# Sparse attention block: one panel's three steps moved between the stretches of a hand-written order

## The chip, the cores and the metric

The kernel runs on one core of one Trainium2 chip. The metric is the device time of one execution in microseconds (us). TensorE (PE) does the matrix products and the transposes, VectorE (DVE) and ScalarE (ACT) the elementwise work, GpSimd (POOL) a part of it, and SyncE (SP) issues most transfers. Each engine works through its own queue in the order in which the program was written; semaphores make an instruction wait for another engine.

## What is computed

The reference is a stack of two blocks with two layers each, all for 512 tokens of width 1024. The change lies in the second block, whose layer (it is run twice) is this, cut to what matters here:

```python
proj = h @ w_in
(q, k, v, g_att, qi, ki, wi, z, xbc, dt_raw, gl_att, gl_ssd) = _split_cols(proj, IN_SIZES)
...
# one_block of _dsa_attention, 128 queries at a time
dots = jnp.einsum('bqhd,bsd->bqhs', qib, ki32) * IDX_DIM ** -0.5          # 4 index heads
score = jnp.einsum('bqhs,bqh->bqs', jax.nn.relu(dots), wb)
score = jnp.where(admissible[None], score, NEG)
_, sel = lax.top_k(score, topk)                                           # topk = 128
logits = ...(q, k[sel]) ; p = softmax(logits) ; o = p @ v[sel]            # 8 heads
y_att = (o_att * jax.nn.silu(g_att)) @ w_branch_a
...
xbc = jax.nn.silu(_causal_dwconv(xbc, conv_w, conv_b))                    # 12 chunks of 128 columns
y = _ssd_chunked(...)
```

## The kernel before

All arrays are kept transposed, 128 columns of a projection on the partitions and the 512 tokens along the free axis. Weights stream through a ring in **panels**: a panel is the 128 output columns of one projection chunk, 8 tiles of 128x128. Each panel is split into a high part (L566, always on ACT) and a low part (L570, on DVE or on POOL), and multiplied in three products per tile, so one panel is 24 matmuls `bank<-hT,wparts 128x512` (L458) into one PSUM bank. `pe_linear_steps` cuts these into three **steps** of 9, 9 and 6 matmuls.

Each layer of the second block (`block2`) has one long stretch in which three **strands** are interleaved. Every strand gives each engine a sequence of steps.

- Strand 0, the projections: four query panels (13 steps), one step for the time constants, five convolution panels (15 steps), then the seven late convolution panels woven with six small steps of `before` (27 steps: the transposes `nat`, the product `last` that reads `rstd`, and for each of two groups the products `cb`, four 128x128 blocks, and the transposes `bn`), then four gate panels (12 steps), and last one step `late_silu`, on ACT alone. A convolution panel costs ACT its start (L1136) and DVE three taps (L1145, together one tap set), a gate panel costs ACT one copy (L2378). `late_silu` is a table load, seven activations (L2140) and four (L2143).
- Strand 1, the selection: for query tiles 1 to 3 the index scores (L2201 on ACT, L2216 and L2219 on DVE) and the search for the 128 largest, which is 16 **rounds** of MAX8 and MATCH_REPLACE8 (L2232, L2234) on DVE for each tile and a mask (L2238) at its end. The width of a round is 256, 384 and 512 for tiles 1, 2 and 3.
- Strand 2, the attention (`softmax_maps`): 32 **maps**, eight heads for each of four query tiles, 128, 256, 384 and 512 keys wide, in 35 steps. PE computes the scores of two maps at once (`bank<-arena 64x..`, then the mask products with `cb_sb`), DVE takes the maximum (L831), ACT the exponential (L819), PE transposes (L468), ACT copies the transposed map out of PSUM (L811; for every fourth map DVE does it, L843), PE multiplies by the values (`last_bank<-arena`), and DVE scales the result out of its single bank (L857). Scores and transposes share four banks, so the scores of a pair wait until both exponentials of the pair before are done. The masks of tile 1 are needed from map 8 on, those of tile 2 from map 16, those of tile 3 from map 24.

The order of the strands is written out by hand as a list of strand numbers. `alternate` walks through it and takes the next step of that strand on all four engines at once; `spread(a, b, c)` deals out a, b and c steps of strands 0, 1 and 2 evenly over a stretch. All the engines' queues follow from this list. The stretches are: four pairs of steps, then the index scores with the search for tile 1 and four rounds of that for tile 2 (strands 0 and 1 only), then the rest of the search for tile 2 beside the maps 0 to 7 (**stage A**), then the search for tile 3 beside the maps 8 to 15 (**stage B**), then the last nineteen map steps (**stage C**).

After the stretch `pe_ot` (L468) transposes the attention output and waits for the last map's result (`"out", 31`); DVE multiplies it with the gates (L2447), then comes `pe_ssd`, which transposes `xbc` into banks that DVE drains (L2561).

Of the kernel before, what the change touches and what calls it, by code (L numbers as in the profile page):

```python
# [253 lines left out]
def spread(*counts):  # L254

    return [i for _, i in sorted(((step + 0.5) / n, i) for i, n in enumerate(counts) for step in range(n))]


def alternate(order, *parts):

    def program(functions):
        def run(eng):
            steps = [f(eng) if f else (i for i in ()) for f in functions]
            for i in order:
                next(steps[i], None)
            for rest in steps:
                finish(rest)
        return run
    return [program([p[i] if i < len(p) else None for p in parts]) for i in range(4)]
# [84 lines left out]
def build(nc, ins, out, known=None, final=False):  # L354
# [9 lines left out]
    with ExitStack() as ctx:  # L364
# [809 lines left out]
        def then(parts=None, **kw):  # L1174
            if parts is not None:
                for e, f in zip(("act", "pe", "dve", "pool"), parts):
                    prog[e].append(f)
            for e, f in kw.items():
                prog[e].append(f)
# [499 lines left out]
        order = [PROJECT, PROJECT, PROJECT, COMPRESS, COMPRESS] * 4  # L1679
# [288 lines left out]
        order = [0, 0, 0] + spread(6, 8) + spread(9, 8) * (KD - 2) + [0] + [1] * (len(maps) + 3)  # L1968
# [55 lines left out]
        def block2(l, nxt, hfree, arena_free):  # L2024
# [404 lines left out]
            rounds, ahead = TOPK // 8, 4  # L2429
            first = 3 * len(later) + 2 + 3 * EARLY - 4  # L2430
            order = [1, 0] * 4 + spread(first, 8 + rounds + ahead)
            order += spread(3 * 5 + 4, rounds - ahead, 8) + spread(3 * 4 + 2, rounds, 8) + spread(3 * 2 + 1, 0, 19)
            then(alternate(order, *strands))

            def pe_ot(pe):
# [355 lines left out]
            return mg  # L2791

        block2(0, Norm("L1h", 0), filled[("f1", "b"), FC - 1], filled[("f1", "y"), KD - 1])
        mg1 = block2(1, None, filled["L0gls", KD - 1], filled["L0out", KD - 1])

        A = Area()
# [209 lines left out]
```

## Time and profile before

| | us |
|---|---|
| median of 3 runs | 2464.34 (2463.07 to 2464.41) |
| profiled execution, its own time | 2462.13 |
| its span on the core | 2460.3 |
| PE busy | 2391.7 (97% of the span) |
| DVE busy | 1423.8 (58%) |
| ACT busy | 1019.4 (41%) |
| POOL busy | 273.9 (11%) |

The median lies 4.0 us above the span and 2.2 us above the profiled execution. The interleaved stretch of the first of the two layers is at 1480 to 1646 us, that of the second about 510 us later. PE is busy nearly all the time, so what can be won or lost is the time in which it waits, plus the time in which its clock is granted at half.

### The profile page before, as it was taken

The numbers are of one execution on the slowest core, as the hardware profiler recorded it, in microseconds if no ns is written. First come the engines' busy times: TensorE is split into PE (matmuls) and PEld (weight loads), VectorE is DVE, ScalarE is ACT, GpSimd is POOL, SyncE is SP. The second block draws the span as 40 slices with busy tenths as digits, with TensorE's granted clock in tenths as the row PEclk, the third lists the DMA queues.
The fourth block names the chain that finished last, engine by engine and source line by source line (L and its number), as shares of the span: only waits on it lengthen the run. The fifth ranks groups of instructions, "written<-read, shape, count | busy, mean of one in ns | idle before, by whom it ended". The sixth has DMA issues, their size and how long they took to land.

```text
span 2460.3 us, 32007 instructions
## 1 busy us (share of the span) xinstructions
PE 2391.7 (97%) x12074; PEld 1925.8 (78%) x12086; DVE 1423.8 (58%) x2366; ACT 1019.4 (41%) x1732; POOL 273.9 (11%) x260
## 2 busy tenths in 40 slices
PE   8999999999999999999999999989999999999998
PEld 7877788888887888788888866777888777678886
DVE  3545655655655666566456469947533578566333
ACT  3656654322334444443233334444422354445223
POOL 0000111000000000100000236302100233011001
PEclk9999999999999999999999999999999999999999
DMA  5211002433432111134334312201232221102321
GB/s 205 87 51 44 1 27 97 152 141 115 147 124 91 60 57 56 61 111 146 145 112 150 107 60 69 69 27 39 92 97 92 79 74 61 43 27 78 103 95 52
DMA packets 58039, 211.77 MB, mean 86 GB/s; under 512 B 6432, under 2 KB 6560, under 8 KB 57888
## 3 DMA queue, kind: packets, MB, share of 16 engines
q1 hardware_dynamic: 57456, 208.86, 24.7%
q8 instruction: 99, 1.62, 0.3%
q10 hardware_dynamic: 432, 0.85, 0.1%
q14 instruction: 52, 0.43, 0.1%
HBM read 207.60 MB, written 2.10 MB: 85 GB/s over the span
## 4 chain that ended last, share of the span: by engine, by line
PE 84%; DVE 6%; issue 4%; ACT 4%; POOL 1%; DMA 0%; SPq 0%; ACTq 0%; DVEq 0%; POOLq 0%
PE bank L458 77%; PE last_bank L458 5%; PE bank L468 3%; DVE arena L1145 1%; DVE arena L2232 1%; ACT wparts L566 1%; DVE arena L2234 1%; DVE small L831 1%; ACT arena L819 1%; POOL rstd L625 0%; DVE wparts L570 0%; DMA ring<-weights_dram 0%; ACT arena L2140 0%; DVE arena_r L584 0%; DVE arena L1006 0%
## 5 line engine op out<-in xcount | busy, mean ns | idle before, releaser
L458 PE MATMUL bank<-hT,wparts 128*128 128x512 f32 x5568 | 1341.3, 397 | 6.9 <-ACT hT L693 4.5
L458 PEld LDWEIGHTS bank<-hT,wparts 128*128 128x128 f32 x5568 | 1038.2, 189 | 239.8 <-issue 24.9
L570 DVE TENSOR_TENSOR wparts<-ring,wparts 128x1024 fp32r<-128x1024 f32 x290 | 366.7, 1265 | 427.0 <-ACT wparts L566 426.8
L458 PE MATMUL bank<-arena_r,wparts 128*128 128x512 f32 x2400 | 566.1, 396 | 0.0
L458 PEld LDWEIGHTS bank<-arena_r,wparts 128*128 128x128 f32 x2400 | 450.1, 188 | 108.4 <-DVE arena_r L600 0.3
L566 ACT ACTIVATE wparts<-ring 128x1024 fp32r<-128x1024 f32 x332 | 348.2, 1049 | 162.1 <-PE bank L458 130.9
L819 ACT ACTIVATE arena<-bank,small 128x128 f32<-128x128 f32 (+3 forms) x192 | 100.9, 526 | 143.0 <-DVE small L831 141.8
L468 PE MATMUL bank<-cf_sb,arena 128*128 128x128 f32 (+1 forms) x816 | 132.8, 281 | 16.7 <-DMA cf_sb<-cf_dram 4.9
L458 PE MATMUL last_bank<-arena 128*128 128x64 f32 x972 | 133.0, 273 | 7.3 <-DVE arena L854 3.1
L458 PEld LDWEIGHTS last_bank<-arena 128*128 128x128 f32 x972 | 124.2, 195 | 16.1 <-issue 9.8
L831 DVE TENSOR_REDUCE small<-bank 128x1 f32<-128x128 f32 (+3 forms) x192 | 93.3, 486 | 57.8 <-PE bank L458 46.2
L570 POOL TENSOR_TENSOR wparts<-ring,wparts 128x1024 fp32r<-128x1024 f32 x42 | 101.1, 2409 | 213.1 <-ACT wparts L566 213.1
L468 PEld LDWEIGHTS bank<-cf_sb,arena 128*128 128x128 f32 (+1 forms) x816 | 96.9, 148 | 32.4 <-DVE arena L1006 5.1
L596 ACT ACTIVATE arena_r<-arena 128x512 fp32r<-128x512 f32 x68 | 42.9, 631 | 179.9 <-POOL arena L2785 93.7
L625 POOL TENSOR_TENSOR rstd<-hv 128x512 f32<-128x512 f32 x6 | 7.8, 1294 | 939.8 <-ACT hv L615 939.8
L458 PE MATMUL bank<-arena 128*64 128x128 f32 (+6 forms) x708 | 91.4, 329 | 14.0 <-ACT arena L819 13.6
L811 ACT ACTIVATE arena<-bank 128x384 f32<-128x384 f32 (+3 forms) x136 | 58.0, 426 | 112.4 <-PE bank L468 111.6
L1136 ACT ACTIVATE arena<-arena,vecs 128x512 f32<-128x512 f32 x44 | 36.0, 817 | 147.3 <-DVE arena L1821 147.3
L458 PEld LDWEIGHTS bank<-arena 128*128 128x128 f32 (+2 forms) x708 | 63.5, 170 | 29.6 <-ACT arena L819 16.2
L1145 DVE SCALAR_TENSOR_TENSOR arena<-arena,vecs 128x511 f32<-128x511 f32 x88 | 66.0, 751 | 16.6 <-ACT arena L1136 15.1
L458 PE MATMUL bank<-cb_sb 128*128 128x128 bf16 (+2 forms) x372 | 74.5, 256 | 0.2
L1821 DVE TENSOR_TENSOR arena<-bank,rstd 128x512 f32<-128x512 f32 x44 | 30.4, 691 | 66.6 <-PE bank L458 62.2
(274 smaller groups left out, 2103.4 us busy)
## 6 DMA issues: line engine op xcount, KB each, us to landing
ring<-weights_dram SPq DMA_DIRECT2D x388, 512.0 KB, 3.4
arena<-x_dram SPq DMA_DIRECT2D x4, 512.0 KB, 5.8
out_dram<-arena SPq DMA_DIRECT2D x4, 512.0 KB, 4.0
rot<-rot_dram SPq DMA_DIRECT2D x1, 512.0 KB, 10.4
rot<-rot_dram ACTq DMA_DIRECT2D x1, 512.0 KB, 3.2
cf_sb<-cf_dram SPq DMA_DIRECT2D x1, 416.0 KB, 8.8
cb_sb<-cb_dram SPq DMA_DIRECT2D x1, 264.0 KB, 9.6
vecs<-vec_dram ACTq DMA_DIRECT2D x1, 258.5 KB, 6.1
```

Source lines behind the costliest of these rows:

```text
L458: i = pe.matmul(*args, **kw)
L468: i = pe.transpose(*args)
L566: eng.activation(wparts[:, slot, 0, :, :], ring[:, p % RAW, :, :], ACT.Copy)\
L570: eng.tensor_tensor(wparts[:, slot, 1, :, :], ring[:, p % RAW, :, :], wparts[:, slot, 0, :, :].bitcast(F32), ALU.subtract)\
L596: act.activation(dst, src, ACT.Copy).then_inc(*act_made.mark((key, "hi")))
L811: act.activation(PT[:, j % 3, 0:W], banks[key, "t", j][:, 0:W], ACT.Copy)\
L819: act.activation(Pb[:, i % 3, 0:W], banks[key, "s", i][:, 0:W], ACT.Exp, bias=mx(i), accum_out=sm(i)).then_inc(*act_made.mark((key, "p", i)))
L831: dve.tensor_reduce(mx(i), banks[key, "s", i][:, 0:W], AX.X, ALU.max, negate=True)\
L1136: act.activation(cv, src, ACT.Identity, bias=b, scale=w).then_inc(*act_made.mark((key, "tap", n)))
L1145: dve.scalar_tensor_tensor(out=cv[:, s:SEQ], in0=src[:, 0:SEQ - s], scalar=w, in1=cv[:, s:SEQ], op0=ALU.mult, op1=ALU.add)\
L1821: dve.tensor_tensor(an[:, n % 3, :], banks[(key, "a"), n][:, :], scale, ALU.mult)\
L2232: dve.max(tops[:, r, :], sc).then_inc(*dve_made.mark((K + "top", qt, r)))
```

## The change

One line of the order list. The four counts of strand 0 over the stretches were 25, 19, 14 and 7; they are now 25, 22, 14 and 4. Three steps, which is one panel, leave stage C and enter stage A. Since strand 0 is a sequence, everything behind its 48th step shifts: stage A takes three more steps of the woven part, stage B begins three steps later in that sequence and takes nine gate steps in place of six, and stage C has three gate steps and `late_silu` in place of six and `late_silu`.

```diff
-            order += spread(3 * 5 + 4, rounds - ahead, 8) + spread(3 * 4 + 2, rounds, 8) + spread(3 * 2 + 1, 0, 19)
+            order += spread(3 * 6 + 4, rounds - ahead, 8) + spread(3 * 4 + 2, rounds, 8) + spread(3 * 1 + 1, 0, 19)
```

In PE matmuls of width 512 the stages held 120, 87 and 48; now they hold 135, 96 and 24. No instruction is added or removed.

**PE, the start of stage A.** Before, the second score pair (`bank<-arena 128x128 x2`) and a transpose stand ahead of the product `last` (`bank<-rstd,cf_sb`):

```order
L458 MATMUL bank<-hT,wparts 128x512 x24
L458 MATMUL bank<-arena 128x128 x2
L458 MATMUL bank<-cb_sb 128x128 x2
L468 MATMUL bank<-cf_sb,arena 128x128
L458 MATMUL bank<-rstd,cf_sb 128x64
L458 MATMUL bank<-hT,wparts 128x512 x6
L468 MATMUL bank<-cf_sb,arena 128x128
L458 MATMUL last_bank<-arena 128x64
```

Now:

```order
L458 MATMUL bank<-hT,wparts 128x512 x24
L458 MATMUL bank<-rstd,cf_sb 128x64
L458 MATMUL bank<-arena 128x128 x2
L458 MATMUL bank<-cb_sb 128x128 x2
L468 MATMUL bank<-cf_sb,arena 128x128
L458 MATMUL bank<-hT,wparts 128x512 x24
L468 MATMUL bank<-cf_sb,arena 128x128
L458 MATMUL last_bank<-arena 128x64
```

The score pair now stands behind `last`, and 24 matmuls of projection stand between two map steps where 6 stood.

**DVE, the end of stage A.** Before, the fifth tap set of the late panels comes behind the mask of tile 2 (L2238):

```order
L831 TENSOR_REDUCE small<-bank 128x1
L836 RECIPROCAL small<-small 128x1
L843 COPY arena<-bank 128x128
L857 TENSOR_SCALAR arena<-last_bank,small 128x64
L2232 MAX arena<-arena 128x8
L2234 MATCH_REPLACE arena<-arena 128x384
L2238 TENSOR_SCALAR arena<-arena 128x384
L1145 SCALAR_TENSOR_TENSOR arena<-bank,vecs,arena 128x511
L1145 SCALAR_TENSOR_TENSOR arena<-bank,vecs,arena 128x510
L1145 SCALAR_TENSOR_TENSOR arena<-bank,vecs,arena 128x509
```

Now:

```order
L1145 SCALAR_TENSOR_TENSOR arena<-bank,vecs,arena 128x511
L1145 SCALAR_TENSOR_TENSOR arena<-bank,vecs,arena 128x510
L1145 SCALAR_TENSOR_TENSOR arena<-bank,vecs,arena 128x509
L2232 MAX arena<-arena 128x8
L2234 MATCH_REPLACE arena<-arena 128x384
L831 TENSOR_REDUCE small<-bank 128x1
L836 RECIPROCAL small<-small 128x1
L843 COPY arena<-bank 128x128
L857 TENSOR_SCALAR arena<-last_bank,small 128x64
L2232 MAX arena<-arena 128x8
L2234 MATCH_REPLACE arena<-arena 128x384
L2238 TENSOR_SCALAR arena<-arena 128x384
```

A tap set has moved ahead of the mask, and behind the mask comes a round of the next search.

**ACT, the end of stage C.** Before, both last copies of transposed maps (maps 30 and 31, `x2`) stand ahead of `late_silu`:

```order
L819 ACTIVATE arena,small<-bank,small 128x512
L2378 ACTIVATE arena<-bank 128x512
L819 ACTIVATE arena,small<-bank,small 128x512
L811 ACTIVATE arena<-bank 128x512 x2
L2140 ACT_TABLE_LOAD
L2140 ACTIVATE arena<-arena 128x512 x7
L2143 ACTIVATE arena<-arena 128x512 x4
L566 ACTIVATE wparts<-ring 128x1024
```

Now:

```order
L819 ACTIVATE arena,small<-bank,small 128x512 x2
L811 ACTIVATE arena<-bank 128x512
L2140 ACT_TABLE_LOAD
L2140 ACTIVATE arena<-arena 128x512 x7
L2143 ACTIVATE arena<-arena 128x512 x4
L811 ACTIVATE arena<-bank 128x512
L566 ACTIVATE wparts<-ring 128x1024
```

The copy of map 31 now stands behind the whole of `late_silu`. Both layers are ordered alike.

## Rows read from the trace of the kernel before

**Rows 1.** The page, part 1: busy time, share of the span, instructions

```profile
PE 2391.7 (97%) x12074; PEld 1925.8 (78%) x12086; DVE 1423.8 (58%) x2366; ACT 1019.4 (41%) x1732; POOL 273.9 (11%) x260
```

**Rows 2.** PE's waits, total, times, longest: 1520 to 1660, then 2032 to 2172

```profile
PE bank L458 <- ACT arena L819: 6.8, 7, 2.0
...
PE bank L458 <- ACT arena L819: 6.7, 7, 2.0
```

**Rows 3.** Windows: busy PE, PEld, DVE, ACT, POOL; clock; DMA; stages A, B, C

```profile
1522.08:1562.79 40.71, 36.93 (x188) 28.75 (x187) 34.50 (x89) 20.55 (x42) 14.82 (x9) 0.96 0.16 54
1562.79:1597.33 34.54, 31.41 (x165) 24.56 (x164) 33.57 (x83) 12.14 (x30) 9.41 (x4) 0.95 0.19 62
1597.33:1646.66 49.33, 44.12 (x279) 33.23 (x280) 21.24 (x60) 23.58 (x55) 0.00 (x0) 1.00 0.10 33
```

**Rows 4.** Timeline of PE in stage A: start, us, instruction, idle before

```profile
1536.25 0.40 PE L458 MATMUL bank<-rstd,cf_sb 16*128 16x64 f32 x2 [3.20 <-DVE arena L1145]
...
1554.72 4.36 PE L458 MATMUL bank<-hT,wparts 128*128 128x512 f32 x18
```

**Rows 5.** Timeline of DVE: tap set, mask, round, ninth maximum, low part

```profile
1554.44 2.32 DVE L1145 SCALAR_TENSOR_TENSOR arena<-bank,vecs,arena 128x511 f32<-128x511 f32 x3 [2.19 <-ACT arena L1136]
...
1561.27 1.45 DVE L2238 TENSOR_SCALAR arena<-arena 128x384 bf16<-128x384 f32 x1
...
1566.83 0.68 DVE L2232 MAX8 arena<-arena 128x8 f32<-128x512 f32 x1
...
1569.74 0.42 DVE L831 TENSOR_REDUCE small<-bank 128x1 f32<-128x256 f32 x1
...
1622.03 1.23 DVE L570 TENSOR_TENSOR wparts<-ring,wparts 128x1024 fp32r<-128x1024 f32 x1 [1.24 <-ACT wparts L566]
```

**Rows 6.** Timeline of PE: score pairs of maps 8, 10, 12, 14 and 18

```profile
1562.79 0.70 PE L458 MATMUL bank<-arena 64*128 64x256 f32 x4
...
1570.90 0.77 PE L458 MATMUL bank<-arena 64*128 64x256 f32 x4 [1.99 <-ACT arena L819]
...
1580.49 0.70 PE L458 MATMUL bank<-arena 64*128 64x256 f32 x4
...
1589.52 0.70 PE L458 MATMUL bank<-arena 64*128 64x256 f32 x4 [1.14 <-ACT arena L819]
...
1603.39 0.92 PE L458 MATMUL bank<-arena 64*128 64x384 f32 x4 [1.35 <-ACT arena L819]
```

**Rows 7.** Timeline of PE: score pairs of maps 22, 26, 28 and 30

```profile
1612.78 0.92 PE L458 MATMUL bank<-arena 64*128 64x384 f32 x4 [0.31 <-ACT arena L819]
...
1624.81 1.13 PE L458 MATMUL bank<-arena 64*128 64x512 f32 x4 [1.27 <-ACT arena L819]
...
1631.15 1.13 PE L458 MATMUL bank<-arena 64*128 64x512 f32 x4
...
1635.98 1.13 PE L458 MATMUL bank<-arena 64*128 64x512 f32 x4 [0.35 <-ACT arena L819]
```

**Rows 8.** Timeline of ACT: copy of map 31, then the step `late_silu`

```profile
1643.67 0.60 ACT L811 ACTIVATE arena<-bank 128x512 f32<-128x512 f32 x1 [0.95 <-PE bank L468]
1644.29 1.28 ACT L2140 ACT_TABLE_LOAD   x1
1645.58 3.75 ACT L2140 ACTIVATE arena<-arena 128x512 f32<-128x512 f32 x7
1649.24 2.17 ACT L2143 ACTIVATE arena<-arena 128x512 f32<-128x512 f32 x4
```

**Rows 9.** Timeline of PE: values of map 31, transposes behind the maps

```profile
1645.21 1.08 PE L458 MATMUL last_bank<-arena 128*128 128x64 f32 x8 [0.47 <-DVE arena L857]
1646.66 6.59 PE L468 MATMUL bank<-cf_sb,arena 128*128 128x128 f32 x44 [0.38 <-DVE arena L857]
1654.28 0.66 PE L468 MATMUL bank<-cf_sb,arena 128*128 128x128 f32 x4 [1.02 <-DVE arena L2561]
```

**Rows 10.** Windows of PE alone: busy, granted clock, after the wait of rows 6

```profile
1572.00:1574.00 2.00, 2.00 (x8) 0.50 0.00 0
```

## Prediction

> **What bounds the kernel now.** The page's busy shares come first: PE is busy 97% of the span, the others far less [rows 1]. The amount of work doesn't change, so the time can change only by PE's waits and by stretches in which its clock is granted at half. Next I looked for PE's waits in the interleaved stretch; the list of waits names the exponentials of ACT as the largest, 6.8 us in seven waits in one layer and 6.7 us in the other [rows 2], so the two layers may be treated alike. Then the windows by stage. In A, PE is busy 36.93 of 40.71 us and DVE 34.50; in B, PE 31.41 of 34.54 and DVE 33.57, 97%; in C, PE 44.12 of 49.33 and DVE only 21.24 [rows 3]. So DVE ends the waits in B, in A both are close, and C is a chain of short dependences between PE, DVE and ACT in which projection matmuls fill holes. The change takes 24 matmuls out of C, puts 15 into A and 9 into B.
>
> **The unit.** 18 projection matmuls last from 1554.72 to 1558.92, where the next instruction starts, 4.2 us [rows 4], so 0.233 us each and 5.6 us for a panel.
>
> **Stage A: 4.9 us longer on PE, mask 5.5 us later.** PE waits 3.20 us for a bank that a tap set must drain, until 1536.25 [rows 4]. That tap set hangs on earlier work of ACT and POOL that keeps its order, so I leave 1536.25 where it is; the score pair that now comes behind the wait (0.55 us, from 1532.23 to 1532.78 by the same timeline) is work moved behind it. From there to the scores of map 8 PE now has 102 matmuls of width 512, 23.8 us; 1.7 us lost to the half clock that follows this wait as it does now; and small pieces of 6.0 us: `last`, three score pairs at about 0.6, two `cb` products at 0.86, `bn` at 0.4, five transposes with values at 0.25. That ends at 1567.7, where it ended at 1562.79 [rows 6]: 4.9 later, made of 3.5 for 15 matmuls, 0.86 for a `cb` that comes forward, 0.55 for the score pair. DVE gets a fifth tap set in this stage, 2.2 us, and idles more, since each tap set waits for ACT's convolution start and that for the end of PE's panel: already now one such wait is 2.19 us [rows 5]. The panels end on PE at 1553.6 and 1560.7; the fifth tap set starts 0.8 us behind the latter, at 1561.5. Behind it come a round (1.2), the small operations of a map (0.65), a round (1.24) and the mask (1.45), all with the durations of now. The mask ends at 1568.25, where it ended at 1562.7 [rows 5].
>
> **Stage B and the first pair of C: 0.8 us shorter (bounds 1.3 and 0.3).** DVE leads here. Behind the mask stand a round of width 512 (1.5), a tap set (2.2), a map's maximum and small operations (0.6), two rounds (2.9, from 1566.83 to 1569.74 [rows 5]). The ninth maximum so starts at 1575.45. Now the scores of map 10 start 1.16 us behind it (1569.74 to 1570.90 [rows 5, 6]); then they start at 1576.6. PE alone could start them at 1574.05 (8.11 us less the wait of 1.99, three more matmuls, `bn` in place of `cb`). So the wait grows from 1.99 to about 2.55. The next tap set needs a panel that PE ends at 1579.5 to 1580.5 and starts at 1580.3 to 1581.3; with two rounds and 1.16 behind it the scores of map 12 start at 1586.6 to 1587.6. To those of map 14 it is 9.03 us now with 1.14 of wait [rows 6]; DVE has one tap set less between them, so I take 7.9. Then 7.8 as now, and to the scores of map 18 6.06 less the wait of 1.35, since the low part that stood between the two maxima (1.23 us on DVE [rows 5]) has moved ahead of them: 4.7. They start at 1607.0 to 1608.0, for 1603.39: **+3.6 to +4.6**, I take +4.1.
>
> **Stage C from map 18 on: -6.0 us.** The 24 matmuls leave, -5.6. What a pair costs bare is shown by two cycles that have no filler: the pair of map 22 waits 0.31 us, that of map 30 0.35 us and comes 4.83 us behind that of map 28 [rows 7]. Four cycles will be bare where two are, so about 0.7 us of new wait. In return the wait of 1.27 us before map 26 goes [rows 7]: it came from a panel's high part on ACT and low part on DVE in that cycle, which now stand elsewhere; and one of 0.40 us before map 24, where ACT's gate copy stood ahead of the exponential. Sum -5.6 + 0.7 - 1.67, which is -6.6; by walking the pairs one by one I get -6.0 and take that. Bounds -5.0 (a bare cycle costs twice as much) and -6.6.
>
> **The end of C: +3.2 us.** `late_silu` lasts from 1644.29 to 1651.41, 7.1 us, and the copy of map 31 stood ahead of it [rows 8]; now it stands behind. Count from the scores of map 30. Now, with six matmuls between (1.4 us, which are gone), the copy of map 30 ends at 6.7, so 5.35 without them. `late_silu` then ends at 12.5, the copy at 13.0, PE takes the values of map 31 at 13.15, having stood from 7.35 on: **a new wait of 5.8 us**. The transposes of `pe_ot` start 1.45 us behind the values (1645.21 to 1646.66 [rows 9]), at 14.6. Of 44 transposes each takes 0.11 us unless it waits, 4.9, so the next four come at 19.5; before they came at 18.3 (1654.28 less 1635.98 [rows 7, 9]), less 1.4. That is +2.6. Why so little: those transposes already ran behind `late_silu`, since the gate products, the low part and the drains of DVE come behind it, and PE waits 1.02 us for that at 1654.28 [rows 9]. The other bound is the half clock. A wait of 1.99 us is enough today for 0.50 in the window behind it, in which eight matmuls take two microseconds [rows 6, 10]; a wait of 5.8 us should do so too, and half-rate transposes add up to 1.1: +3.7. I take +3.2.
>
> **Sum.** Per layer 4.1 - 6.0 + 3.2 = +1.3, for two layers +2.6. The span goes from 2460.3 to 2462.9, the median, 4.0 above it, from 2464.3 to **2466.9**.
>
> **A rule of the Trainium skill that speaks for more.** The trace shows 1.28 us for the table load in `late_silu`, and the first activation starts 0.01 us behind it [rows 8]; nothing stands between the copy's end and the load either. The Trainium skill, "ScalarE: Activation LUTs", section What ACT_TABLE_LOAD costs, adds a drain of about 1.38 us to a load of 1.28 for each switch. By that rule, an estimate, the copy of map 31 would come 1.4 us later per layer and the sum would be +5.4 in place of +2.6. The trace contradicts it for this load.
>
> **Rivals.**
>
> *The holes of A and B take the panel (faster).* If DVE idles less in A than I count, the three waits of 1.99, 1.14 and 1.35 [rows 6] vanish, together with the half clock behind the first (1.7 us). A and B then cost 5.6 - 4.5 - 1.7 = -0.6, the layer -0.6 - 6.0 + 3.2 = -3.4, the kernel 2457.5. For it: PE's share of work grows between the maps, so DVE has more time for each maximum. Against: the fifth tap set stands ahead of the mask, and DVE is busy 97% of B [rows 3].
>
> *DVE carries its whole delay through B (slower).* The mask is 5.5 us late. If B costs DVE all of its 35.5 us again (the tap set that left, 2.2, is made up by the low part, 1.2, and by the wait for the panel, 1.0 or more) the scores of map 18 start 6 us late in place of 4.1; with -5.0 in C and +3.7 at its end the layer is +4.7, the kernel 2473.7. It decides once DVE waits more than about 2 us for the tap set at 1580. For it: every stage has its own slowest engine now, PE in A and DVE in B, and what one gives up the other doesn't take. Against: B needs 34.4 us of DVE where it needed 35.5.
>
> *The change doesn't hurt the tail.* If the copy of map 31 isn't waited for, because the transposes behind it are held by something else anyway, the layer is 4.1 - 6.0 = -1.9 and the kernel 2460.5. Against it stands the order alone: `pe_ot` waits for the output of map 31, and PE can't go around it.
>
> **How the numbers follow.** The forecast as summed, within the bounds of its terms (3.6 - 6.6 + 2.6 = -0.4 to 4.6 - 5.0 + 3.7 = +3.3 a layer, 2463.5 to 2471), has 0.6. The slower rival has 0.22, the faster one 0.1, the harmless tail 0.08. The table rule lies within the forecast's range and has 0.05 of those 0.6. About 0.2%, 4.9 us, is what a measurement of this kernel can tell from no change: 2459.4 and 2469.3 are the borders. Of the forecast a sixth lies above 2469.3, with the slower rival 0.3; the faster rival lies almost wholly below 2459.4, and so does a sliver of the harmless tail, 0.1; 0.6 remains for no difference. The range goes from 2461.5, which leaves out the faster rival and some of the harmless tail, to 2472.5, which takes in half of the slower one.
>
> **What would show it.** In the changed profile: the scores of map 8 about 5 us later and the mask of tile 2 5 to 6 us later; a wait of 2 to 3 us before the scores of map 10; no wait over 0.5 us before those of maps 24 and 26; the scores of map 18 3.6 to 4.6 us later; and a wait of 5 to 6 us on PE for ACT's L811 once per layer, with a window at 0.50 near it. The prediction is wrong in its first part if the wait before map 10 is gone, in its last if the wait behind map 30 is short. The three terms have opposite signs and each is larger than their sum, so the sign of the whole is its weakest part.

## The result

The changed kernel takes 2471.94 us (median of 8 runs, 2467.45 to 2476.75), the kernel before 2464.38 us (8 runs, 2463.07 to 2465.94) in the same comparison. The ratio is 1.003 with a 95% interval from 1.0021 to 1.0039: slower by 7.6 us. The forecast was 2466.9, with a range from 2461.5 to 2472.5; it called a difference under 0.2% the likeliest, and that is not what came. The measured time lies inside the range, 0.6 us below its upper end.

The profiled execution of the changed kernel took 2467.45 us, which is its fastest run. Its span is 2465.6 us. The page, part 1, for [rows 1]:

```profile
PE 2388.7 (97%) x12086; PEld 1922.9 (78%) x12086; DVE 1424.6 (58%) x2366; ACT 1019.6 (41%) x1732; POOL 273.9 (11%) x260
```

As before, PE is busy 97% of the span, and these shares don't show the change. The list of PE's waits of the interleaved stretch, first layer, does (engine, line waited for: total, times, longest; for [rows 2]):

```profile
PE last_bank L458 <- ACT arena L811: 5.7, 1, 5.7
PE bank L458 <- ACT arena L819: 5.3, 7, 1.3
PE bank L458 <- DVE arena L1145: 4.5, 2, 4.0
```

The waits for exponentials fell from 6.8 to 5.3 us, and a single wait of 5.7 us for a copy (L811) is new. Windows of the changed kernel (columns as in [rows 3]): from the first score pair to that of map 8, from there to map 18, to map 30, and to the first matmul of the next panel behind the maps:

```profile
1519.27:1564.60 45.33, 40.80 (x211) 32.55 (x210) 36.99 (x92) 21.30 (x43) 17.05 (x9) 0.96 0.21 71
1564.60:1604.97 40.37, 36.23 (x192) 27.47 (x191) 35.66 (x89) 16.63 (x39) 7.18 (x3) 1.00 0.16 54
1604.97:1632.87 27.90, 25.91 (x168) 18.64 (x168) 13.50 (x40) 13.01 (x34) 0.00 (x0) 1.00 0.06 21
1632.87:1656.19 23.32, 17.21 (x111) 15.31 (x111) 9.53 (x20) 11.17 (x20) 1.03 (x1) 0.78 0.05 15
```

The last three of these stretches of the kernel before (the first is the first of [rows 3], 40.71 us):

```profile
1562.79:1603.39 40.60, 36.12 (x191) 28.08 (x191) 37.25 (x91) 15.68 (x38) 9.41 (x4) 0.96 0.21 67
1603.39:1635.98 32.59, 29.63 (x183) 21.85 (x186) 13.95 (x40) 13.95 (x35) 0.00 (x0) 1.00 0.09 31
1635.98:1655.07 19.09, 17.02 (x116) 14.66 (x117) 8.77 (x19) 11.79 (x21) 1.03 (x1) 0.91 0.03 6
```

I call these four stretches A, B', C' and the end in what follows; B' reaches one pair further than B, to map 18. The differences are +4.62, -0.23, -4.69 and +4.23 us: +3.9 for the layer, and by the same marks +4.1 in the second layer, 8.0 together. The two spans differ by only 5.3, since the execution of before that was profiled came 2.8 us later to the start of the stretch (1522.08 against 1519.27), where both kernels are alike. A second profile of the changed kernel has the stretch start at 1525.15, takes 137.05 us for the layer in place of 136.92, and has a span of 2471.6. So the sum over the layers, not the difference of two spans, is what answers to the medians. The same marks in all thirteen profiles bear this out: what comes behind the second of these stretches takes 293.9 us in each (293.85 to 293.99), while the first stretch, which the same program precedes in all, starts anywhere from 1519.27 to 1525.29.

### The profile page after: what moved, and what is told of

It is laid out like the page before. It is cut to its first block, busy times and chain, and to the rows that moved or that the text cites. A ratio compares the mean times of both kernels' runs of the same rounds, so it can differ in the third digit from the quotient of the medians.

```text
span 2465.6 us, 32019 instructions
## 1 busy us (share of the span) xinstructions
PE 2388.7 (97%) x12086; PEld 1922.9 (78%) x12086; DVE 1424.6 (58%) x2366; ACT 1019.6 (41%) x1732; POOL 273.9 (11%) x260
## 4 chain that ended last, share of the span: by engine, by line
PE 84%; DVE 6%; issue 4%; ACT 4%; POOL 1%; DMA 0%; SPq 0%; ACTq 0%; DVEq 0%; POOLq 0%
PE bank L458 76%; PE last_bank L458 4%; PE bank L468 3%; DVE arena L1145 1%; DVE arena L2232 1%; DVE arena L2234 1%; DVE small L831 1%; ACT arena L819 1%; ACT wparts L566 0%; POOL rstd L625 0%; DMA ring<-weights_dram 0%; DVE wparts L570 0%; ACT arena L2140 0%; DVE arena_r L584 0%; ACT arena L1136 0%
## 5 line engine op out<-in xcount | busy, mean ns | idle before, releaser
L570 DVE TENSOR_TENSOR wparts<-ring,wparts 128x1024 fp32r<-128x1024 f32 x290 | 366.7, 1265 | 427.3 <-ACT wparts L566 427.1
L570 POOL TENSOR_TENSOR wparts<-ring,wparts 128x1024 fp32r<-128x1024 f32 x42 | 101.2, 2412 | 206.0 <-ACT wparts L566 205.9
L811 ACT ACTIVATE arena<-bank 128x384 f32<-128x384 f32 (+3 forms) x136 | 57.9, 426 | 102.5 <-PE bank L468 101.7
L1145 DVE SCALAR_TENSOR_TENSOR arena<-arena,vecs 128x511 f32<-128x511 f32 x88 | 66.0, 750 | 16.6 <-ACT arena L1136 15.1
```

The lines of the kernel that those rows point to most:

```text
L570: eng.tensor_tensor(wparts[:, slot, 1, :, :], ring[:, p % RAW, :, :], wparts[:, slot, 0, :, :].bitcast(F32), ALU.subtract)\
L811: act.activation(PT[:, j % 3, 0:W], banks[key, "t", j][:, 0:W], ACT.Copy)\
L1145: dve.scalar_tensor_tensor(out=cv[:, s:SEQ], in0=src[:, 0:SEQ - s], scalar=w, in1=cv[:, s:SEQ], op0=ALU.mult, op1=ALU.add)\
```

## The end of C in the changed kernel

Timeline of PE, from the scores of map 30 on (start, us, instruction, idle before; for [rows 9]):

```profile
1632.87 1.13 PE L458 MATMUL bank<-arena 64*128 64x512 f32 x4 [0.35 <-ACT arena L819]
...
1639.37 1.08 PE L458 MATMUL last_bank<-arena 128*128 128x64 f32 x8
1646.10 1.97 PE L458 MATMUL last_bank<-arena 128*128 128x64 f32 x8 [5.65 <-ACT arena L811]
1648.44 7.99 PE L468 MATMUL bank<-cf_sb,arena 128*128 128x128 f32 x48 [0.38 <-DVE arena L857]
1656.19 4.14 PE L458 MATMUL bank<-hT,wparts 128*128 128x512 f32 x17
```

And ACT beside it, for [rows 8]:

```profile
1637.84 0.60 ACT L811 ACTIVATE arena<-bank 128x512 f32<-128x512 f32 x1 [0.29 <-PE bank L468]
1638.45 1.28 ACT L2140 ACT_TABLE_LOAD   x1
1639.75 3.74 ACT L2140 ACTIVATE arena<-arena 128x512 f32<-128x512 f32 x7
1643.40 2.17 ACT L2143 ACTIVATE arena<-arena 128x512 f32<-128x512 f32 x4
1645.47 0.57 ACT L811 ACTIVATE arena<-bank 128x512 f32<-128x512 f32 x1
```

PE stands from the values of map 30 until the copy of map 31, which is queued behind all of `late_silu`. The eight matmuls of map 31 then take 1.97 us where those of map 30 took 1.08, and the 48 transposes take 7.99. The windows of PE alone, for [rows 10], inside the wait, behind it in three places, and in the next panel (length, busy, granted clock, DMA share, GB/s):

```profile
1644.00:1646.00 2.00, 0.00 (x0) 0.50 0.00 0
1646.40:1648.40 2.00, 1.67 (x8) 0.50 0.03 8
1648.40:1651.40 3.00, 2.96 (x14) 0.50 0.00 0
1651.40:1654.40 3.00, 3.00 (x19) 0.62 0.00 0
1654.60:1657.60 3.00, 3.00 (x23) 1.00 0.52 175
```

The clock is at its lower level, 1.2 GHz (0.50; the upper one is 2.4 GHz, 1.00), already within the wait and stays there through most of the transposes: 14 of them in three microseconds. So the order of ACT's queue costs twice: the wait, and the work behind it at half rate.

## Experiments

Ahead of each result stands what was written before that run. The runs came in three groups, each with its own runs of the kernel before; their medians are 2463.9 (the changed kernel once more, both moves of `late_silu`, the filled wait), 2464.2 (the panel from C into B, both moves of rounds, 16, 14, 10) and 2464.8 (the last three). Differences are taken within a group.

### The changed kernel once more

> The changed kernel once more, as the partner of the three runs beside it. In its profile the layer is 3.9 us longer than before: +4.4 up to the scores of map 18, -5.9 from there to the end of map 30's values, +5.4 from there to the first z panel. My theory (the copy of map 31 behind late_silu, and the half clock that the 5.65 us wait brings) expects about +8 us on the median, that is 2472, and each layer's stretch with the clock at 0.50 near the end of the maps. The rival theory (what costs is the delay of DVE in the stages A and B) expects the same time but for another reason.

2472.59 us (5 runs), ratio 1.0035 [1.0022, 1.0048], 8.7 above before. The result repeats. The profiled run of these is the one of 2471.6 us of span named above.

### The same order with late_silu behind the last map step

```diff
             order += spread(3 * 6 + 4, rounds - ahead, 8) + spread(3 * 4 + 2, rounds, 8) + spread(3 * 1 + 1, 0, 19)
+            order += [order.pop(len(order) - 1 - order[::-1].index(0))]
```

> The changed order with its last projection step (late_silu) put back behind the last map step; only ACT's order differs from the changed kernel. My theory: the wait of 5.65 us before the values of map 31 is gone, from the end of map 30's values to the first z panel it takes 10.3 us again instead of 15.7, a layer is 4.4 - 5.9 = -1.5 against before, the kernel 2461.4 us (2460 to 2463), 3 us faster than before. The rival (A and B carry the loss): 2468 to 2472, since nothing in A and B differs from the changed kernel.

2463.47 us (11 runs), ratio 0.9996 [0.9988, 1.0005]: 9.1 us below the changed kernel, though the panel is still in A. That is 0.5 above its range, of which the ledger below tells, and far from the rival's 2468. The end of this kernel on PE, whose scores of map 30 start at 1637.25:

```profile
1646.76 1.97 PE L468 MATMUL bank<-cf_sb,arena 128*128 128x128 f32 x16 [0.38 <-DVE arena L857]
1649.68 3.50 PE L468 MATMUL bank<-cf_sb,arena 128*128 128x128 f32 x28 [0.96 <-ACT arena L2140]
1654.38 0.66 PE L468 MATMUL bank<-cf_sb,arena 128*128 128x128 f32 x4 [1.20 <-DVE arena L2562]
1655.18 5.72 PE L458 MATMUL bank<-hT,wparts 128*128 128x512 f32 x24
```

The transposes still wait for `late_silu` (0.96 and 1.20 us), but sixteen of them run before that wait, at full rate, and the end takes 17.93 us in place of 23.32. A and B' are as long as in the changed kernel. The whole slowdown hangs on which of two ACT steps comes first.

### The kernel before with late_silu ahead of the copy of map 31

```diff
             order += spread(3 * 5 + 4, rounds - ahead, 8) + spread(3 * 4 + 2, rounds, 8) + spread(3 * 2 + 1, 0, 19)
+            order.insert(len(order) - 3, order.pop(len(order) - 2))
```

> The order of before with late_silu put one map step earlier, so that the copy of map 31 stands behind it; nothing is moved between the stages. My theory: PE waits 5 to 6 us before the values of map 31 in each layer, and with the half clock a layer is 5.4 us longer: 2464.4 + 10.8 = 2475 us (2470 to 2477). The rival: the transposes behind the maps wait for late_silu anyway, so at most +1 a layer, 2464 to 2466.

2472.84 us (5 runs), ratio 1.0039 [1.0026, 1.0051]. This is the end of the change alone, with every panel where it was:

```profile
1652.65 1.97 PE L458 MATMUL last_bank<-arena 128*128 128x64 f32 x8 [5.65 <-ACT arena L811]
1655.00 7.39 PE L468 MATMUL bank<-cf_sb,arena 128*128 128x128 f32 x48 [0.38 <-DVE arena L857]
```

The same wait of 5.65 us and the same 1.97. Against the same kernel with `late_silu` last this order alone costs 9 us, within the theory's range and far from the rival's 1 us a layer. By the layer it costs 4.8 us here (23.91 for 19.09) and 5.4 in the changed kernel (23.32 for 17.93): the values come as late in both, but here the clock is back earlier, and from the transposes to the next panel it is 7.15 us in place of 7.75.

### The wait filled with matmuls

For map 31 (`fill_at=31` in the call for these 32 maps) PE takes the bank of its values first, then runs 26 matmuls into it whose results nobody reads (they are overwritten), then waits for the copy. The order of the other engines is that of the changed kernel.

```diff
-        def softmax_maps(..., together=False, busy=0):
+        def softmax_maps(..., together=False, busy=0, fill_at=None):
...
+                        if j and j == fill_at:
+                            bank = banks.take(pe, (key, "o", j), out)
+                            pe_busy(pe, bank, 26)
...
-                        if j:
+                        if j and j != fill_at:
```

> The changed kernel with 26 matmuls of width 512 (bf16, result overwritten) put on PE into the wait before the values of map 31, so that PE has work in it; they add no time unless they last longer than the wait of 5.65 us. Theory of the clock (half of the loss at the end of the maps is the half clock that the wait brings): no window at 0.50 behind the maps, the end of stage C costs 2.6 to 3 us instead of 5.4, the kernel 2466.5 us (2465 to 2468). The rival, that the order alone costs the 5.4: the kernel stays at 2472.

2466.02 us (11 runs), ratio 1.0014 [1.0005, 1.0023], 6.6 us below the changed kernel, with work added. Its end on PE, and the window over its transposes:

```profile
1644.37 5.56 PE L458 MATMUL last_bank<-cb_sb 128*128 128x512 bf16 x25 [0.61 <-DVE arena L860]
1649.76 1.00 PE L458 MATMUL last_bank<-arena 128*128 128x64 f32 x8
1651.14 5.69 PE L468 MATMUL bank<-cf_sb,arena 128*128 128x128 f32 x48 [0.38 <-DVE arena L860]
1656.98 1.40 PE L458 MATMUL bank<-hT,wparts 128*128 128x512 f32 x5
```

```profile
1651.20:1656.20 5.00, 4.99 (x45) 1.00 0.00 0
```

(The trace has 25 of the 26; a few matmul records can be missing from a trace.) ACT's copy comes as late as before, and the values of map 31 start even later, 13.58 us behind the scores of map 30 for 13.23, since the last of the filler is still running. But from there to the transposes it is 1.38 us in place of 2.34, and from the transposes to the next panel 5.84 in place of 7.75. The instructions and their number are the same and the clock is 1.00 in place of 0.50, so the half clock costs 1.0 and 1.9, together 2.9 us a layer. The end takes 20.80 us (1636.18 to 1656.98) in place of 23.32. The rest of the end's cost is the order itself: 23.32 less 2.9 and less the 17.93 with `late_silu` last, 2.5 us a layer.

### The panel from C into B

```diff
-            order += spread(3 * 5 + 4, rounds - ahead, 8) + spread(3 * 4 + 2, rounds, 8) + spread(3 * 2 + 1, 0, 19)
+            order += spread(3 * 5 + 4, rounds - ahead, 8) + spread(3 * 5 + 2, rounds, 8) + spread(3 * 1 + 1, 0, 19)
+            order += [order.pop(len(order) - 1 - order[::-1].index(0))]
```

> The panel leaves stage C as in the change, but goes wholly into stage B (19, 17 and 4 steps of strand 0), and late_silu stands behind the last map step. Stage A is that of the kernel before. Theory (the cost of the change ahead of the scores of map 18 comes from putting the panel into A, in front of the mask): A stays at 40.7 us, B takes the panel partly into its three waits of 1.99, 1.14 and 1.35 us, so from the scores of map 8 to those of map 18 it is 42 to 43.5 us where it is 40.6 before; C loses 5.9, its end nothing. The layer is 2 to 4 us shorter than before, the kernel 2456 to 2460. Rival (a panel costs its full 5.6 us wherever it stands, since maximum, exponential and search form one chain whose waits come back): B is 46 us, the kernel 2463 to 2465, like the change with late_silu last.

2457.03 us (6 runs), ratio 0.9971 [0.9959, 0.9982]: faster than before by 7.1 us and than the changed kernel by 15, as its theory says; the rival's 2463 to 2465 didn't come. The windows of B' and the end (A and C' are in the ledger):

```profile
1560.22:1603.07 42.85, 40.46 (x216) 31.21 (x215) 38.20 (x92) 16.85 (x40) 9.35 (x4) 1.00 0.22 74
1630.96:1648.88 17.92, 14.70 (x111) 11.93 (x111) 8.67 (x19) 11.30 (x20) 1.03 (x1) 1.00 0.03 5
```

B' had 4.48 us of idle PE (40.60 less 36.12) and a mean clock of 0.96; now it has 2.39 idle and the full clock. Of the panel's 5.6 us only 2.25 show: 2.1 went into idle time, and the rest, 1.3, is what the full clock gives back. A keeps its length, and C' saves the same 4.7 as in the change.

### Two rounds of the third search from B into A

The changed kernel with `late_silu` last, and then the kernel before, each with `rounds - ahead + 2` and `rounds - 2` in the first two stretches. PE's order doesn't change by it.

> The changed kernel with late_silu behind the last map step, and two of the sixteen rounds of the search for tile 3 (1.45 us of DVE each) moved from stage B into stage A, whose PE order stays as it is. Theory (DVE leads in B, PE in A): in A DVE is busy 37.0 of 45.3 us and takes the 2.9 us into its idle time, so A grows by 0 to 1 us; in B the three waits of 1.3, 1.3 and 1.15 us shrink by 2 to 2.9 us together. The layer is 1 to 2.9 us shorter, the kernel 2458 to 2461.5 where it is 2463.5 without this edit. Rival (DVE's work from the start of A to the end of B is one chain with the panels, and a round costs the same wherever it stands): no change, 2462.5 to 2464.5; or the mask and the first maxima of B come 2.9 us later and the kernel is 2465 to 2469.

> The kernel before with the same edit as the run before this but one: two rounds of the search for tile 3 moved from stage B into stage A. Theory (DVE leads in B already before the change): in A DVE has 6.2 us of idle time and PE 3.8; A grows by 0.5 to 2 us, B loses 2 to 2.9 of its 4.5 us of waits, the layer is 0 to 2 us shorter, the kernel 2460 to 2464. If DVE's work in A and B is one chain, nothing changes, 2464. If this edit gains less here than on the changed kernel, the panel in A has indeed given DVE idle time there that it lacks before.

On the changed order 2463.47 us (11 runs), ratio 0.9993 [0.9984, 1.0002], where 2463.47 was measured without the edit; on the order of before 2462.46 (11 runs), ratio 0.9995 [0.9986, 1.0003]. The windows of B' in the changed order without the two rounds' move, and with it:

```profile
1568.95:1609.36 40.41, 36.24 (x192) 27.47 (x191) 35.69 (x89) 16.65 (x39) 7.19 (x3) 1.00 0.17 54
```

```profile
1569.46:1610.02 40.56, 36.18 (x192) 27.48 (x192) 34.07 (x84) 16.52 (x39) 7.18 (x3) 1.00 0.17 55
```

DVE is busy 1.6 us less, not the 2.9 of two rounds, and B' doesn't get shorter. Part of the difference is the mask of tile 2, which took 0.36 us in the changed order and takes 1.52 here (the last section comes back to it). The mask, and two waits in B', one of PE and one of DVE:

```profile
1562.85 1.52 DVE L2238 TENSOR_SCALAR arena<-arena 128x384 bf16<-128x384 f32 x1
...
1574.82 0.41 PE L458 MATMUL last_bank<-arena 128*128 128x64 f32 x2 [1.30 <-DVE arena L857]
...
1582.36 2.32 DVE L1145 SCALAR_TENSOR_TENSOR arena<-bank,vecs,arena 128x511 f32<-128x511 f32 x3 [1.97 <-ACT arena L1136]
```

The tap set at 1582.36 waits 1.97 us for its panel, where the same one waits 1.05 in the changed kernel: DVE had time to spare there. And PE waits 1.30 us for a small operation of DVE (L857) where it had no wait. On the order of before:

```profile
1564.20:1603.88 39.68, 34.76 (x191) 26.88 (x191) 34.25 (x85) 15.68 (x38) 9.41 (x4) 1.00 0.20 66
```

DVE is busy 3.0 us less than in B' of before and the stretch is 0.92 shorter, while the clock goes from 0.96 to 1.00 and PE's busy time falls by 1.36. A did not grow but fell by 0.23. The time lies in the range of its theory, but not for its reason: B' should have lost 2 to 2.9 us of waits. So the total of DVE's work doesn't set the length of B'. On the changed order the time is that of the rival, no change; its reason, one unbroken chain of DVE's work, doesn't fit the 1.97 us in which DVE stands idle. The mask blurs both tests by 1.1 us, since it got longer by that in the one and shorter in the other.

### More and other panels

Counts of strand 0 over A, B and C, `late_silu` last in all three: 16, 14, 10; then 19, 20, 1; then 16, 20, 4.

> The opposite move: one panel leaves stage A and enters C (16, 14 and 10 steps of strand 0 where before has 19, 14 and 7), late_silu behind the last map step. Theory (A has PE as its slowest engine, C is a chain with holes): C takes 5.6 us of matmuls, of which 0.7 to 1 fill bare pairs, so +4.5 to +5.5; in A and B the scores of map 18 come 3 to 4.4 us earlier, less than a panel, since DVE is busy 34.5 of 40.7 us in A and 97% of B. The layer is 0.5 to 2 us longer than before, the kernel 2465 to 2468. Rival (the exchange is even, as between before and the changed kernel with late_silu last): 2463 to 2465.

> One more panel leaves stage C for stage B (19, 20 and 1 steps of strand 0, late_silu last; the version with 19, 17 and 4 gave 2457.0). Theory (a panel is cheap only while the stage that takes it has idle time on PE, and worth removing only while its stage isn't bare): B has 2.4 us of idle PE left in 42.85, so the panel adds 4.5 to 6 us there; C loses only 2 to 3 us, since then all of its pairs are bare chains of 3.7 to 4.9 us. The layer is 1.5 to 4 us longer, the kernel 2460 to 2465. Rival (the gain of 7 us repeats, B still hides part of it): 2450 to 2456.

> One panel from C and one from A both into stage B (16, 20 and 4 steps of strand 0, late_silu last). Theory (idle PE time in B is used up by the first panel): A takes 37.3 us as in the run with 16 steps there, 3.4 less than with 19; B takes 47 to 48.5 where it is 42.85; the layer is 0.7 to 2.2 us longer than with 19, 17 and 4, the kernel 2458 to 2462. Rival (B is the stage with room, and a panel costs less there than anywhere else): 2453 to 2456.5.

They take 2467.36 us (11 runs), ratio 1.0013 [1.0004, 1.0021]; 2458.53 us (9 runs), 0.9979 [0.9970, 0.9989]; and 2458.04 us (11 runs), 0.9973 [0.9964, 0.9982]. None is below 2457.03, though the last two, measured in another group, can't be told from it. The first lies in its expectation as a whole, with both parts smaller: C' grew by 4.2 (4.5 to 5.5 expected), and the scores of map 18 came 2.7 earlier (3 to 4.4). The third has A and B' as its theory says (37.32 and 47.76). The second is better than its theory's 2460 to 2465 and short of its rival's 2450 to 2456. Its B':

```profile
1564.87:1610.90 46.03, 43.70 (x231) 34.16 (x230) 38.79 (x92) 17.69 (x41) 9.44 (x4) 1.00 0.24 81
```

C' fell by 2.41, to 25.48, as expected, and has no panel left. But B' grew by 3.2 and not by 4.5 to 6, because I had counted 24 matmuls where 15 enter it (231 instructions on PE for 216): the nine of the first step of C stand between the maps 16 and 18 already and so within B'. 15 matmuls of 0.233 are 3.5 us; B' hid next to nothing of them, and C' gave back 2.4 for them, 1.1 less than they take.

### The panel in B, late_silu in the changed kernel's place

> Steps 19, 17 and 4 of strand 0, but late_silu ahead of the last map step as in the changed kernel. Theory (the cost of the end of C is independent of where the panel went): the new wait of 5.7 us, half clock for 10 us behind it, 3.5 to 4.6 us a layer, so 7 to 9 us above the version with late_silu last: 2464 to 2466. Rival (late_silu costs little when ACT arrives early at the end of C): under 2461.

2465.75 us (11 runs), ratio 1.0004 [0.9995, 1.0013], 8.7 above the version with `late_silu` last, in the range of its theory. The wait of 5.65 us and the half clock come wherever the panel goes; the end costs 4.8 us here (22.70 for 17.92), as on the order of before, where it is 5.4 in the changed kernel.

### The ledger

All in us, first layer; the two columns on the right are both layers together and the measured medians, each less before.

| counts of A, B, C | `late_silu` | A | B' | C' | end | layer | two layers | measured |
|---|---|---|---|---|---|---|---|---|
| 19, 14, 7 (before) | last | 40.71 | 40.60 | 32.59 | 19.09 | 132.99 | 0 | 0 |
| 22, 14, 4 (the change) | early | 45.33 | 40.37 | 27.90 | 23.32 | 136.92 | +8.0 | +7.6 |
| 22, 14, 4 | last | 45.33 | 40.41 | 27.89 | 17.93 | 131.56 | -2.4 | -0.4 |
| 19, 14, 7 | early | 40.76 | 40.60 | 32.58 | 23.91 | 137.85 | +8.9 | +9.0 |
| 22, 14, 4, wait filled | early | 45.36 | 40.43 | 27.89 | 20.80 | 134.48 | +2.3 | +2.1 |
| 19, 17, 4 | last | 40.73 | 42.85 | 27.89 | 17.92 | 129.39 | -7.1 | -7.1 |
| 19, 17, 4 | early | 40.74 | 42.84 | 27.89 | 22.70 | 134.17 | +1.8 | +1.0 |
| 22, 14, 4, rounds moved | last | 45.69 | 40.56 | 27.89 | 17.93 | 132.07 | -1.7 | -0.7 |
| 19, 14, 7, rounds moved | last | 40.48 | 39.68 | 32.59 | 19.09 | 131.84 | -2.3 | -1.7 |
| 16, 14, 10 | last | 37.30 | 41.34 | 36.75 | 19.09 | 134.48 | +2.2 | +3.2 |
| 19, 20, 1 | last | 40.73 | 46.03 | 25.48 | 17.95 | 130.19 | -5.6 | -6.2 |
| 16, 20, 4 | last | 37.32 | 47.76 | 27.89 | 17.92 | 130.89 | -4.8 | -6.7 |

The measured +7.6 of the change is that of the first comparison; its repetition gave +8.7 with a ledger of +8.2. Ledger and measured medians agree within 1.0 us, but for two rows. 16, 20, 4 is 1.9 better than its ledger, which stays unexplained. 22, 14, 4 with `late_silu` last is 2.0 worse; there the trace shows 1.6 us more at a place outside the stretch. From the first panel behind the end to the first score pair of the second layer it takes 379.3 us, and the version with the filled wait 377.8. At one place in that part its clock is half for a while, and in the other version it isn't (PE alone; both windows lie in the same run of 18 projection matmuls, which takes 6.00 us in the first version and 4.37 in the second):

```profile
1973.00:1976.00 3.00, 3.00 (x9) 0.55 0.00 0
```

```profile
1973.00:1976.00 3.00, 3.00 (x16) 1.00 0.00 0
```

The waits just ahead of that place are equal in both (0.68 us the longest). Why the clock falls in the one and not in the other isn't settled. Both versions with two rounds moved show it too, at the same place (0.53), also that on the order of before, whose PE order is that of the kernel before, which doesn't show it. Their medians are 1.0 and 0.6 above their ledgers, so this place explains the 2.0 only in part, and one profile of each doesn't tell how often it occurs.

## Why the prediction was right or wrong, point by point

**Stage A: right in size, not in each part.** The scores of map 8 come 4.62 us later, counted from the first score pair, for 4.9. PE's wait ahead of `last` is longer than I left it:

```profile
1533.43 0.40 PE L458 MATMUL bank<-rstd,cf_sb 16*128 16x64 f32 x2 [3.96 <-DVE arena L1145]
```

3.96 for the 3.20 of [rows 4]; `last` itself starts where it did, 14.16 us behind the first pair, as I had assumed. The end of the mask of tile 2 is 4.5 us later, for 5.5. With the 1.45 us of [rows 5] it would have been 5.6, but it didn't take them:

```profile
1564.03 0.36 DVE L2238 TENSOR_SCALAR arena<-arena 128x384 bf16<-128x384 f32 x1
```

**Stage B: the sum was right, the steps were not.** I took the wait ahead of the scores of map 10 to grow to 2.55 us; it shrank to 1.30. I took the mask to be on the path, with its long duration. The scores of map 12 came 5.2 us late by the same count, under the 6.1 to 7.1 forecast, and B' as a whole 0.23 shorter, so the scores of map 18 are 4.39 late for +4.1, bounds 3.6 and 4.6. That the sum fits is luck, for two errors offset each other: the half clock of [rows 10] disappeared with the shorter wait, and a wait of 1.15 us stood ahead of map 18, for which I had taken off the whole wait of before. Another, of 1.31, stood ahead of map 12, whose start I had left to DVE:

```profile
1572.56 0.70 PE L458 MATMUL bank<-arena 64*128 64x256 f32 x4 [1.30 <-ACT arena L819]
...
1582.91 0.70 PE L458 MATMUL bank<-arena 64*128 64x256 f32 x4 [1.31 <-ACT arena L819]
...
1599.75 0.92 PE L458 MATMUL bank<-arena 64*128 64x384 f32 x4 [1.15 <-ACT arena L819]
```

The premise "DVE leads in B, 97% busy" fell, as far as it meant the total of DVE's work, in the two runs with moved rounds. A busy share near one on an engine that does small steps in a fixed order says that it has little slack, not that its total sets the stage's length. That the waits follow from which piece of DVE stands ahead of which maximum fits the traces, where they move with the order; no run tests a single such place.

**Stage C: right.** From the scores of map 18 to the end of the values of map 30 it is 5.87 us less, for -6.0. The terms written out gave -6.6; the walk that led to -6.0 isn't shown, so how well its parts fit can't be told. For [rows 7]:

```profile
1612.61 0.92 PE L458 MATMUL bank<-arena 64*128 64x384 f32 x4 [0.32 <-ACT arena L819]
...
1622.40 1.13 PE L458 MATMUL bank<-arena 64*128 64x512 f32 x4 [0.56 <-ACT arena L819]
```

The wait ahead of map 24 went, that ahead of map 26 fell from 1.27 to 0.56, where I said none over 0.5.

**The end of C: the step that failed.** The wait came as forecast, 5.65 us for 5.8, and the values of map 31 start 13.23 us behind the scores of map 30, for 13.15. But the term was +3.2, bounds 2.6 and 3.7, and it measured +5.4 (end of the values of map 30 to the next panel: 10.33 before, 15.74 now). The order alone was sized right: 2.5 us by the runs, for 2.6. I gave the half clock between 0 and 1.1 us, by counting it on the transposes only and on a part of them; it costs 2.9. The values of map 31, at half rate, put 1.0 more between them and the transposes, which I had left out, since I copied the 1.45 us of [rows 9] from full rate. And the transposes cost 1.9 more.

I took the price of half clock from a place where it follows a wait of 1.99 us and is short. Before the change there is a second such place, which I didn't use, right behind the maps:

```profile
1646.66:1649.66 3.00, 3.00 (x14) 0.50 0.00 0
1649.90:1652.90 3.00, 3.00 (x30) 1.00 0.00 0
```

The transposes ran at half rate for the first three microseconds there, free of charge, and that without a long wait ahead of them (0.47 us the longest behind the scores of map 26): with that half clock 8.41 us pass from the first transpose to the next panel, and in the version of 22, 14, 4 with `late_silu` last, without it, 8.42. They wait for `late_silu` anyway. In the change `late_silu` is done, nothing hides the half rate any more, and it goes on through most of 10 us of work.

**The sum.** +4.4, -5.9 and +5.4 make +3.9 a layer for the forecast +1.3. Two of three large terms were right, and the error of the third, 2.2 us a layer, is larger than the whole sum. That is what the last lines of the prediction warned of. The bound for the third term was too narrow, not the idea wrong. And it is luck that the time lies in the range: the bounds of the three terms end at 2471, and 2471.94 is inside only because the range was stretched to take in half of the slower rival, whose mechanism didn't come.

**The rivals.** The time of the second rival, 2473.7, is near the measured one, but by another mechanism: DVE did not carry its whole delay through B (4.39 in place of 6). The harmless tail is refuted by the run with `late_silu` last. The holes of A and B did not take the panel: PE's idle time in A went from 3.78 to 4.53 us. With the panel in B alone the three waits and the half clock behind the first do vanish, as that rival has it, but a wait of 1.52 us for a tap set appears, and A and B' cost +2.3 us, not its -0.6.

**The table load.** The rule of the Trainium skill ("ScalarE: Activation LUTs", section What ACT_TABLE_LOAD costs) adds a drain of about 1.38 us, and would by my estimate have put the sum at +5.4 in place of +2.6. The trace of the changed kernel shows none of it: the copy of map 30 ends at 1638.44, the load starts at 1638.45 and takes 1.28, and the activation starts at 1639.75. That its sum is nearer to the measured one is chance.

## What to carry to other kernels

When work is moved in an order list, look first at what the move drags along at its far end: here the panel itself cost and gave nearly the same, and a long step on ACT that slipped ahead of one short copy decided the sign. Where a wait on PE grows to several microseconds, price the half clock on all the work behind it, and ask whether something else had been hiding it. A panel belongs where PE waits (B' hid 3.4 of its 5.6 us, 1.3 of them through the clock), not where an engine's busy share looks low.

## What was not expected of the hardware

- The clock behind a wait. Behind the 1.99 us of [rows 6] the window of two microseconds at 1572.00 shows 0.50 and the clock is back at 1.00 by 1575.0; behind 5.65 us it is at 0.50 for the values and most of the transposes, from 1646.4 to past 1651.4, on top of the end of the wait itself. With the wait filled by matmuls it is 1.00 over the transposes. But a long wait isn't the only thing that half clock follows: behind the maps of the kernel before it came after 0.47 us, in the ledger's odd place after 0.68.
- The mask on DVE (L2238, 128x384). Before it takes 1.45 us and after 0.36. POOL's low part (L570) lay beside it before:

```profile
1560.09 2.41 POOL L570 TENSOR_TENSOR wparts<-ring,wparts 128x1024 fp32r<-128x1024 f32 x1 [5.61 <-ACT wparts L566]
```

  The mask of before starts at 1561.27, within it, and ends just past it; in the changed kernel POOL is idle from 1562.16 to 1569.96, and the mask starts at 1564.03. The other traces agree without exception: in the 26 layers of the thirteen profiles the mask of this width takes 1.44 to 1.52 us in the 12 in which a low part is running on POOL when it starts, and 0.36 in the 14 in which none is. Moving two rounds on DVE alone switched it both ways, 0.36 to 1.52 on the changed order and 1.45 to 0.36 on that of before. The tap sets (L1145) show nothing of the kind: that at 1562.64, beside the next low part, takes 2.30 us, as elsewhere. The Trainium skill ("GPSIMD Engine Reference", section Specifications) states that GpSimd's SBUF interfaces are shared with VectorE and contend with DVE instructions in a 2-port mode or with two SBUF inputs. The durations agree with such a contention; which mode the mask runs in no run here shows.
- The spread of the same kernel's runs goes with the mean granted clock: the changed kernel's 2467.45 us has 0.992 and its 2476.75 has 0.987. A single profile of it can lie 4.5 us under the median. The two profiles of the changed kernel show where: part of the 5.9 us by which the slower one comes later to the stretch is time at half clock that the faster one hasn't, as here (PE alone; the faster one first):

```profile
280.00:284.00 4.00, 3.50 (x30) 1.00 0.00 0
```

```profile
280.00:284.00 4.00, 4.00 (x20) 0.50 0.00 0
```
